# Two transformer blocks on one core: routing on unscaled rows, a slot table in memory, gather and sum by matrix products, and the second projection in the same program block

## The chip, the cores and the metric

The kernel runs on one core of a Trainium2 chip. The metric is device time in microseconds (us). TensorE does the matrix products (PE in the rows, its weight loads PEld), VectorE (DVE), ScalarE (ACT) and GpSimd (POOL) the elementwise work, and SyncE (SP) issues most transfers. All data are float32.

## The reference

512 tokens of width 1024 pass through two blocks. In each: RMS norm, an input projection, a mixer (stick-breaking attention and RWKV-7 in the first, HGRN2 and forgetting attention in the second), an output projection added to the residual, RMS norm, and a mixture of experts with a two-level router. After the experts there is a final RMS norm; that of the first block feeds the second block. The experts and what stands on both sides of them are what changes:

```
h  = h + mixed @ w_out
xn = rmsnorm(h, norm_ffn_g)
# router: softmax over 4 groups of (xn @ w_grp + b_grp), best group;
#         in it the best two experts of (xn @ w_exp + b_exp), with weights
for e in range(N_EXPERTS):
    y = y + combine[:, e:e+1] * ((silu(xn @ w_gate[e]) * (xn @ w_up[e])) @ w_down[e])
h = rmsnorm(h + y, final_norm_g)
# second block: u = rmsnorm(h, attn_norm_2) @ w_in_2, and so on
```

The first block has 32 experts with a hidden width of 256, the second 16 with 512. Either way a block reads 100.7 MB of expert weights.

## The kernel before

The phases run one after the other, each in a program block of its own with a barrier of all engines behind it: first projection (`phase_project1`), attention, RWKV, the expert block (`expert_block`), second projection (`phase_project2`), HGRN2, forgetting attention, the expert block again.

An expert block is made of three parts. `out_programs` projects with w_out, four token tiles of 128 rows by two halves of 512 columns, on TensorE; VectorE adds to the residual `z.h`; ScalarE squares the row, takes a root, and writes the scaled row `z.xn` in a permuted order of columns, which TensorE turns (`turn`) into `mixT`; TensorE multiplies with the router weights (`route`). A chain of small VectorE instructions picks group and experts, and TensorE counts the rank of each token in its expert (`z.q`).

`moe_programs` (first block) and `wide_programs` (second block) then run eight bodies each. The weights of a body (12.6 MB: four experts or two) stand in one buffer per expert, and a buffer's next load is issued by SP when the body's product with it is done; the gate and up weights are freed by `gate_up`, the down weights by `down`. A body's 256 slots (four experts by 64) or 192 slots (two by 96) are found by a one-hot matrix `z.G` on VectorE and a product with the token numbers on TensorE (`index_pe`); GpSimd fetches the rows by an indirect transfer from memory (`fetch_rows`); TensorE turns them (`turn_rows_pe`) and VectorE writes them with the gain (`turned_rows_dve`). Rows of the body after next are fetched while a body runs. ScalarE copies each output and stores all slots, full or empty, in memory (`expert_rows`). The bodies are a hardware loop of six passes and two more behind it; a branch over further rounds, for more tokens than slots, follows.

`final_programs` starts after the last body's stores: GpSimd fetches each token's two rows with eight indirect transfers, VectorE multiplies and adds them, and the final norm follows. After the first block, its result is stored, the engines meet at the barrier, and `phase_project2` norms the rows again, turns them (`norm_turn_pe`) and projects (`project_pe`).

## Time and profile before

| | us |
|---|---|
| median of 3 runs (1667.97 to 1669.82) | 1669.01 |
| the profiled execution, its own time | 1672.01 |
| its span, first to last instruction | 1670.3 |
| mean granted TensorE clock | 0.903 of full |
| PE busy | 1399.1 (84%) |
| DVE busy | 424.3 (25%) |
| ACT busy | 354.1 (21%) |
| POOL busy | 158.4 (9%) |
| moved by DMA | 287.34 MB, mean 172 GB/s |

The busy share of 84% is a mean over stages: the two blocks' stages each have their own limit, and the rows further down are therefore cut by stage. The PE row counts the time in which a product runs, whatever the clock; a product of a 128x128 tile with 512 columns in float32 is two instructions.

### The profile page before, as it was taken

To read this page: it belongs to the slowest core of one execution; us is meant where nothing else is said; L and a number is where in the kernel's file an instruction comes from. 1 tells how busy PE (TensorE), PEld (TensorE's weight loads), DVE (VectorE), ACT (ScalarE), POOL (GpSimd) and SP (SyncE) were. 2 spreads that over 40 slices of the span, in tenths; PEclk is the share of its full clock that TensorE was granted. 3 is DMA by queue.
4 is the path that set the end of the run, shared out by engine and by line. 5 is a ranking of instruction groups with operands and counts; after the bars stand their busy time and mean duration, and the time that the engine had idled before them with its cause. 6 is when DMAs were issued, how large, how long until landed. Compare 5 with 4: busy or idle time off the path is not lost. (4 is left out here: it accounts for less than half of the span.)

```text
span 1670.3 us, 23492 instructions
## 1 busy us (share of the span) xinstructions
PE 1399.1 (84%) x9946; PEld 701.0 (42%) x9946; DVE 424.3 (25%) x827; ACT 354.1 (21%) x615; POOL 158.4 (9%) x217
## 2 busy tenths in 40 slices
PE   5999989877896988778089999577889799999991
PEld 3434444677455433232044444466545433333320
DVE  2234325422214111101421000682512311111003
ACT  2023026342211111101221100323522011111101
POOL 4000002252001001000100000240000000000001
PEclk8989999999995989989599999786999699999996
DMA  5111100200425899998523210002052389989944
GB/s 190 51 51 51 50 0 0 103 4 4 147 100 200 357 419 418 418 416 332 179 105 119 76 51 0 1 1 71 31 216 115 112 336 358 363 347 358 372 186 171
DMA packets 70007, 287.34 MB, mean 172 GB/s; under 512 B 11475, under 2 KB 12570, under 8 KB 57634
## 3 DMA queue, kind: packets, MB, share of 16 engines
q1 hardware_dynamic: 57088, 250.41, 38.5%
q0 software_dynamic: 6400, 16.79, 3.0%
q10 hardware_dynamic: 6434, 18.92, 2.9%
q8 instruction: 64, 1.05, 0.3%
q14 instruction: 21, 0.17, 0.0%
HBM read 269.30 MB, written 23.07 MB: 175 GB/s over the span
## 5 line engine op out<-in xcount | busy, mean ns | idle before, releaser
L344 PE MATMUL banks<-mixT,ring 128*128 128x512 f32 x672 | 294.9, 601 | 3.8 <-DVE mixT L285 3.8
L344 PEld LDWEIGHTS banks<-mixT,ring 128*128 128x128 f32 x672 | 129.3, 193 | 168.6 <-issue 164.4
L1922 PE MATMUL banks<-arena_moe,mixT 128*32 128x512 f32 x768 | 173.7, 600 | 0.0
L1922 PE MATMUL banks<-ring,mixT 128*32 128x512 f32 x768 | 117.2, 617 | 5.7 <-DMA arena_moe<-in_w_up 4.8
L1372 PE MATMUL banks<-ring,mixT 128*128 128x512 f32 x256 | 114.4, 607 | 8.0 <-PEq L51 8.0
L1558 POOL DMA_INDIRECT arena_moe<-normed_rows,arena_moe x32 | 32.8, 1025 | 745.9 <-DVE arena_moe L1586 605.7
L1749 PE MATMUL banks<-arena_moe,mixT 128*64 128x512 f32 x256 | 70.2, 709 | 37.6 <-DMA arena_moe<-in_exp_w_up 37.6
L341 PE MATMUL banks<-ring,mixT 128*128 128x512 f32 x192 | 82.9, 592 | 0.0
L1372 PEld LDWEIGHTS banks<-ring,mixT 128*128 128x128 f32 x256 | 49.4, 195 | 69.5 <-issue 69.5
L1922 PEld LDWEIGHTS banks<-ring,mixT 128*32 128x32 f32 x768 | 34.0, 114 | 86.3 <-issue 86.3
L1749 PE MATMUL banks<-ring,mixT 128*64 128x512 f32 x256 | 60.0, 623 | 6.8 <-DMA ring<-in_exp_w_up 5.6
L1609 DVE TENSOR_TENSOR mixT<-banks,params 128x512 f32<-128x512 f32 (+1 forms) x64 | 38.7, 622 | 102.5 <-PE banks L1600 102.5
L2001 DVE TENSOR_TENSOR mixT<-mixT,banks 128x256 f32<-128x256 f32 x24 | 10.1, 421 | 197.6 <-ACT mixT L2029 197.6
L1922 PEld LDWEIGHTS banks<-arena_moe,mixT 128*32 128x32 f32 x768 | 43.8, 109 | 35.1 <-issue 35.1
L1749 PEld LDWEIGHTS banks<-arena_moe,mixT 128*64 128x64 f32 x256 | 22.9, 162 | 84.7 <-issue 84.7
L1944 PE MATMUL banks<-ring,mixT 128*32 128x512 f32 x384 | 56.5, 594 | 0.5 <-ACT mixT L2033 0.5
L1944 PE MATMUL banks<-arena_moe,mixT 128*32 128x512 f32 x128 | 56.4, 593 | 0.0
L341 PEld LDWEIGHTS banks<-ring,mixT 128*128 128x128 f32 x192 | 36.5, 190 | 45.9 <-issue 45.9
L1600 PE MATMUL banks<-ident,arena_moe 128*128 128x128 f32 (+1 forms) x256 | 49.8, 300 | 6.3 <-DMA arena_moe<-normed_rows,arena_moe 6.3
L2186 ACT ACTIVATE arena_mix<-banks 128x512 f32<-128x512 f32 x28 | 16.7, 597 | 176.8 <-PE banks L344 129.8
L1807 DVE TENSOR_TENSOR mixT<-mixT,banks 128x256 f32<-128x256 f32 x16 | 6.7, 421 | 184.1 <-ACT mixT L1835 184.1
L462 ACT ACTIVATE arena_mix<-banks 128x512 f32<-128x512 f32 x26 | 15.5, 597 | 174.0 <-PE banks L344 148.9
(392 smaller groups left out, 1925.5 us busy)
## 6 DMA issues: line engine op xcount, KB each, us to landing
ring<-in_w_in SPq DMA_DIRECT2D x18, 1024.0 KB, 7.5
arena_moe<-in_exp_w_gate SPq DMA_DIRECT2D x16, 1024.0 KB, 18.8
arena_moe<-in_exp_w_up SPq DMA_DIRECT2D x16, 1024.0 KB, 23.1
arena_moe<-in_exp_w_down SPq DMA_DIRECT2D x16, 1024.0 KB, 21.6
ring<-in_exp_w_gate SPq DMA_DIRECT2D x16, 1024.0 KB, 16.1
ring<-in_exp_w_up SPq DMA_DIRECT2D x16, 1024.0 KB, 18.0
ring<-in_exp_w_down SPq DMA_DIRECT2D x16, 1024.0 KB, 23.0
arena_moe<-in_w_gate SPq DMA_DIRECT2D x8, 2048.0 KB
```

The lines of the kernel that those rows point to most:

```text
L341: last = pe.matmul(bank[:, 0:4 * P], m.mixT[:, c, i * P:(i + 1) * P], w[:, c, 0:4 * P], start=(c == 0), stop=(c == DC - 1))
L344: last = pe.matmul(bank[:], w[:, c, i * P:(i + 1) * P], m.mixT[:, c, :], start=(c == 0), stop=(c == DC - 1))
L462: act.activation(out, bank, ACT.Copy, scale=scale).then_inc(ph.sem("taken"), 1)
L1372: last = pe.matmul(m.banks[k % 3][:], m.mixT[:, c, i * P:(i + 1) * P], w[:, c, :], start=(c == 0), stop=(c == DC - 1))
L1558: pool.indirect_dma_start(z.xs[0:count, c, :], None, z.normed, bass.IndirectOffsetOnAxis(ap=z.index[0:count, c:c + 1].bitcast(U32), axis=0 ...
L1600: last = pe.transpose(pair[a][:, at:at + count], z.xs[0:count, c, j * P:(j + 1) * P], m.ident[0:count, 0:count])
L1609: dve.tensor_tensor(z.xe[:, j:j + 2, :], pair[a][:, 0:2 * z.slots].rearrange("p (j n) -> p j n", j=2), m.params[:, gain + j:gain + j + 2]. ...
L1749: last = pe.matmul(hb[u][k * cap:(k + 1) * cap, :], z.xe[:, j, s * cap:(s + 1) * cap], both[:, :, j, :], start=(j == 0), stop=(j == DC - 1))
L1922: last = pe.matmul(hb[u][T * i:T * (i + 1), :], z.xe[:, j, at:at + T], both[:, :, j, half * 256:half * 256 + 256], start=(j == 0), stop=(j ...
L1944: last = pe.matmul(yb[n][T * i:T * (i + 1), :], z.hT3[:, h, f, T * i:T * (i + 1)], wd[:, 2 * half + f, n * HW:(n + 1) * HW], start=(h == 0 ...
L2001: dve.tensor_tensor(z.hid3[:, u, :], z.hid3[:, u, :], hb[u][:, 256:512], ALU.mult).then_inc(ph.sem("hidden_done"), 1)
L2186: act.activation(out, bank[:], func, scale=scale).then_inc(ph.sem("taken"), 1)
```

## The change

In words, by part:

- **First projection.** GpSimd makes a blank; SP writes two tables of slots and two output arrays of 4.2 MB with it (`clear_exchange`), behind the loads of the third weight item. Two more gain vectors are loaded by ScalarE.
- **Before the experts.** TensorE turns the unscaled rows `z.h`, so `turn` and `route` no longer wait for the row's norm; the gain is multiplied into the router's weights, the scale and the bias are applied to the logits of each tile. ScalarE and VectorE also split the normed row into a rounded part `x_hi` and its rest `x_lo`, in the type F32R.
- **Slots.** The per-body one-hot, `index_pe` and `index_dve` are gone. One one-hot is built for the first body. GpSimd writes, by eight indirect transfers, for each token and choice a pair (row number, weight) into a table in memory; SP reads the whole table back, four transfers in pieces of 8 bytes; GpSimd turns it into row numbers.
- **First body.** TensorE gathers the rows as a product of `x_hi` and `x_lo` with the one-hot (`gather_pe`, 64 products).
- **Bodies 1 to 7.** Rows are fetched by the table. ScalarE applies the weight when it copies the output, and waits for the table before the first body's work. GpSimd scatters the outputs of bodies 0 to 6 by indirect transfers to token order (`place_rows`), only full slots. The bodies are written out; the branch for further rounds now stands ahead of body 0.
- **End.** The outputs of bodies 0 to 6 are loaded in token order while the last body runs (`load_outputs`), VectorE adds them (`early`), the last body's outputs are split into `y_hi` and `y_lo` and summed by TensorE (`sums_pe`, 32 products), and VectorE adds the banks.
- **Second projection** runs in the same program block; its first weights are asked for while the last body runs. `between_programs` computes both norms in one go: two squares, a root and two scaled copies per tile on ScalarE.

The core of the diff:

```
+    pool.memset(x.zeros, 0.0).then_inc(ph.sem("blank"), 1)
+    pool.iota(x.blank, [[0, P], [-NOWHERE, 2]], base=NOWHERE, channel_multiplier=0).then_inc(ph.sem("blank"), 1)
...
+def clear_exchange(sp, ph, x, exchanges):
+
+    sp.wait_ge(ph.sem("blank"), 2)
+    for d in exchanges:
+        sp.dma_start(d.outputs.rearrange("(p a) (b n) -> p (a b) n", p=P, n=512), x.zeros.unsqueeze(1).broadcast_to([P, 16, 512])).then_inc(ph.sem("cleared"), 16)
+        n = d.table.shape[0] // P
+        sp.dma_start(d.table.rearrange("(p n) v -> p n v", p=P), x.blank[:, 0:n, :]).then_inc(ph.sem("cleared"), 16)
...
+            act.wait_ge(ph.sem("cleared"), 32 * len(exchanges))
...
+        parts = m.open(f"moe{block}", {"x_hi": (NT, D), "x_lo": (NT, D), "G": (NT * 256,)})
+        self.x_hi, self.x_lo = parts["x_hi"], parts["x_lo"]
+        self.G = parts["G"][:, 0:NT * self.slots].rearrange("p (t n) -> p t n", t=NT)
+        self.ST = parts["G"][:].rearrange("p (c s) -> p c s", c=2)
...
+        spent = m.ring01[:, 0, 0:NT * D] if self.wide else self.ring23[:, 0, 0:NT * D]
+        self.outs = (spent.rearrange("p (t d) -> p t d", d=D), self.xn)
...
+    def load_slots(self, sp, slots, first_rank, sem):
+
+        t = self.d.table.rearrange("(i e n) v -> e i n v", e=self.EB, n=self.d.entries)
+
+        def part(partition, c, e, rank, n):
+            src = t[e][:, bass.ds(first_rank + rank, n), :].rearrange("i n v -> n i v")
+            sp.dma_start(slots.raw[partition:partition + n, :, c, :], src).then_inc(sem, 16)
+
+        if self.wide:
+            part(0, 0, 0, 0, self.cap)
+            part(self.cap, 0, 1, 64, self.cap - 64)
+            part(0, 1, 1, 0, 64)
+            part(64, 1, 1, 0, 64)
+        else:
+            for e in range(4):
+                part(64 * (e % 2), e // 2, e, 0, 64)
...
+        pe.wait_ge(ph.sem("wr_scaled"), 1)
         for i in range(1, NT):
-            project(i)
-            if i >= 2:
-                route(i - 2)
+            project(i, 0, every)
             turn(i - 1)
-        route(NT - 2)
+            project(i, 1, front)
+            route(i - 1)
+            project(i, 1, back)
         turn(NT - 1)
         route(NT - 1)
 
...
+            act.activation(z.x_hi[:, i, :], z.xn[:, i, :], ACT.Copy).then_inc(ph.sem("high"), 1)
...
+        def split(t_):
+
+            dve.wait_ge(ph.sem("high"), t_ + 1)
+            dve.tensor_tensor(z.x_lo[:, t_, :], z.xn[:, t_, :], z.x_hi[:, t_, :].bitcast(F32), ALU.subtract).then_inc(ph.sem("split"), 1)
...
+        dve.tensor_tensor(z.wr[:, :, 0:G + E], z.wr[:, :, 0:G + E], m.params[:, gain:gain + DC].unsqueeze(2).broadcast_to([P, DC, G + E]),
+                          ALU.mult).then_inc(ph.sem("wr_scaled"), 1)
...
+    def gpsimd(pool):
+
+        pool.iota(z.count, [[1, S]], base=0, channel_multiplier=0).then_inc(ph.sem("ramp"), 1)
+        pool.wait_ge(ph.sem("ramp"), 1)
+        pool.tensor_copy(z.ramp, z.count).then_inc(ph.sem("ramp"), 1)
+        pool.wait_ge(ph.sem("entries"), 2)
+        for t_ in range(NT):
+            for k in range(2):
+                pool.indirect_dma_start(z.d.table, bass.IndirectOffsetOnAxis(ap=z.position[:, k, t_:t_ + 1].bitcast(U32), axis=0),
+                                        z.entry[:, k, t_, :], None, bounds_check=E * z.d.entries - 1,
+                                        oob_is_err=False).then_inc(ph.sem("tabled"), 16)
...
+def gather_pe(pe, ph, z, banks):
+
+    for b in range(4):
+        for j in (2 * b, 2 * b + 1):
+            at = (j % 2) * z.slots
+            for t in range(NT):
+                for part in (z.x_hi, z.x_lo):
+                    last = pe.matmul(banks[b][:, at:at + z.slots], part[:, t, j * P:(j + 1) * P], z.G[:, t, :],
+                                     start=(t == 0 and part is z.x_hi), stop=(t == NT - 1 and part is z.x_lo))
+        last.then_inc(ph.sem("gathered"), 1)
...
+def sums_pe(pe, ph, m, z, t, c, last_part):
+
+    for n in range(2):
+        for part in (z.y_hi, z.y_lo):
+            if z.wide and c == 1:
+                a, b, y = 64 * n, 64 * n + 64, part[64 * n:64 * n + 64, 2, :]
+            else:
+                a, b, y = 0, P, part[:, 2 * c + n, :]
+            last = pe.matmul(m.banks[2 * t + n][:], z.ST[a:b, c, t * P:(t + 1) * P], y,
+                             start=(c == 0 and part is z.y_hi), stop=(c == 1 and part is z.y_lo), skip_group_check=True)
+    if last_part:
+        last.then_inc(ph.sem("summed"), 1)
+
+
+def all_sums_pe(pe, ph, m, z, first, both):
+
+    pe.wait_ge(ph.sem("chosen_slots"), 2)
+    pe.wait_ge(ph.sem("y_low"), first)
+    for t in range(2):
+        sums_pe(pe, ph, m, z, t, 0, False)
+    pe.wait_ge(ph.sem("y_low"), both)
+    for t in range(2):
+        sums_pe(pe, ph, m, z, t, 1, True)
+    for t in range(2, NT):
+        for c in range(2):
+            sums_pe(pe, ph, m, z, t, c, c == 1)
...
+def load_outputs(sp, ph, z):
+
+    sp.wait_ge(ph.sem("hidden"), z.units * (z.bodies - 1) + 2)
+    sp.wait_ge(ph.sem("placed"), 32 * (z.bodies - 1))
+    for t in range(NT):
+        for k in range(2):
+            sp.dma_start(z.outs[k][:, t, :], z.d.outputs[k * S + t * P:k * S + (t + 1) * P, :]).then_inc(ph.sem(f"outputs{t}"), 16)
...
+        sp.wait_ge(out.sem("tabled"), TABLED)
+        z.load_slots(sp, z.main, 0, ph.sem("slots"))
+        further.run(sp, begin, body, lambda n: body(n * NB, 0))
+        load_gain()
+        for i in range(1, NB):
+            for s in range(4):
+                sp.wait_ge(ph.sem("hidden"), 2 * i + s // 2 - 1)
                 z.load_in(sp, io, s, i, ring_sems[s])
             for s in range(4):
-                sp.wait_ge(ph.sem("down"), g * 2 + s // 2 - 1)
+                sp.wait_ge(ph.sem("down"), 2 * i + s // 2 - 1)
                 z.load_down(sp, io, s, i, ring_sems[4 + s])
-
-        with sp.Fori(1, NB) as i:
-            fill(i, i)
-        sp.wait_ge(out.sem("rounds"), 1)
-        n = sp.value_load(m.rounds[0:1, 0:1], min_val=1, max_val=rounds.most)
-        with sp.If(n > 1):
-            with sp.Fori(1, n) as r:
-                with sp.Fori(0, NB) as i:
-                    fill(r * NB + i, i)
-        with sp.Else():
-            sp.nop()
+        load_outputs(sp, ph, z)
...
+        further_pool(pool, further, z, x, out, 4)
+        pool.wait_ge(ph.sem("slots"), 64)
+        slots_known(pool, z, z.main, ph.sem("known"), 0)
+        fetch_rows(pool, ph, z, z.main.fetch[:, 1, :])
+        for i in range(NB - 1):
+            pool.wait_ge(ph.sem("y_taken"), 4 * i + 2)
+            place_rows(pool, ph, z, z.main.place[:, i, :], 0)
+            if i + 2 < NB:
+                pool.wait_ge(ph.sem("gathered"), 4 * (i + 1) + 4)
+                fetch_rows(pool, ph, z, z.main.fetch[:, i + 2, :])
+            pool.wait_ge(ph.sem("y_taken"), 4 * i + 4)
+            place_rows(pool, ph, z, z.main.place[:, i, :], 1)
...
+        chosen_slots_dve(dve, ph, z)
+        hidden(ph, NB - 1, 0)
+        hidden(ph, NB - 1, 1)
+        for c in range(2):
+            for n in range(2):
+                y_low_dve(dve, ph, z, 2 * c + n, yb[2 * c + n], z.main.weight[:, NB - 1, c:c + 1])
+        for t in range(NT):
+            early(t)
...
+        act.wait_ge(ph.sem("slots"), 64)
+        for i in range(NB - 1):
+            hiddens(ph, i)
...
+        def squares(t):
+            act.wait_ge(experts.sem("total"), t + 1)
+            act.activation(store[:, t, :], z.h[:, t, :], ACT.Square, accum_out=stat(t, S1)).then_inc(ph.sem("squares"), 1)
+            act.wait_ge(ph.sem("gained"), t + 1)
+            act.activation(m.rows[:, t, :], hg[:, t, :], ACT.Square, accum_out=stat(t, S2)).then_inc(ph.sem("squares"), 1)
+
+        def root(t):
+            act.wait_ge(ph.sem("means"), t + 1)
+            act.activation(stat(t, D1, 2), stat(t, MS1, 2), ACT.Sqrt).then_inc(ph.sem("deviations"), 1)
+
+        def scale(t):
+            act.wait_ge(ph.sem("inverses"), t + 1)
+            act.activation(scaled[:, t, :], hg[:, t, :], ACT.Copy, scale=stat(t, BOTH)).then_inc(ph.sem("scaled"), 1)
+            act.activation(store[:, t, :], hg[:, t, :], ACT.Copy, scale=stat(t, I1)).then_inc(ph.sem("unscaled"), 1)
+            act.wait_ge(ph.sem("unscaled"), t + 1)
+            act.dma_start(rows[:, t, :], store[:, t, :]).then_inc(ph.sem("stored"), 16)
+
+        for t in range(NT):
+            squares(t)
+            root(t)
+            if t:
+                scale(t - 1)
+        scale(NT - 1)
+        act.wait_ge(ph.sem("stored"), 16 * NT)
+        p_scalar(act)
...
+        for t in range(NT):
+            add_sums_dve(dve, experts, m, z, t)
+            gained(t)
+            if t:
+                means(t - 1)
+            if t >= 2:
+                inverses(t - 2)
+        means(NT - 1)
+        inverses(NT - 2)
+        inverses(NT - 1)
+        dve.wait_ge(ph.sem("squares"), 2 * NT)
+        for t in range(NT):
+            taken(t)
...
```

## Rows read from the trace of the kernel before

**Rows 1.** Windows by stage: PE, PEld, DVE, ACT, POOL busy, clock, DMA share, GB/s.

```profile
564.90:778.70 213.80, 170.54 (x812) 70.00 (x809) 27.17 (x55) 29.54 (x55) 10.98 (x11) 0.91 1.02 418
...
1283.80:1320.90 37.10, 25.11 (x133) 21.47 (x132) 13.21 (x48) 6.37 (x8) 1.99 (x2) 0.57 0.56 213
1320.90:1634.00 313.10, 307.30 (x2560) 104.92 (x2560) 36.46 (x100) 37.01 (x77) 13.61 (x14) 0.95 0.81 313
1634.00:1670.30 36.30, 0.00 (x0) 0.00 (x0) 16.16 (x20) 6.93 (x14) 8.15 (x8) 0.55 0.50 181
```

**Rows 2.** Timeline of block 1 between its projection and its first body.

```profile
499.46 1.87 PE L1392 MATMUL banks<-arena_moe,mixT 128*128 128x36 f32 x16
...
512.60 0.31 DVE L1473 TENSOR_TENSOR arena_moe<-banks,arena_moe 128x144 f32<-128x144 f32 x1 [3.72 <-PE banks L1392]
...
518.44 0.80 PE L1409 MATMUL banks<-arena_moe,after 128*128 128x128 f32 x2 [5.88 <-DVE arena_moe L1491]
...
520.80 1.29 DVE L1801 TENSOR_TENSOR arena_moe<-slots,arena_moe 128x512 f32<-128x512 f32 x2
...
538.05 8.86 PE L1749 MATMUL banks<-ring,mixT 128*64 128x512 f32 x32 [1.20 <-DVE arena_moe L1586]
```

**Rows 3.** TensorE's timeline in block 1: bodies 0, 1 and 7.

```profile
553.98 1.04 PE L1600 MATMUL banks<-ident,arena_moe 128*128 128x128 f32 x8
...
559.68 1.84 PE L1577 MATMUL banks<-tokens,arena_moe 128*128 128x1 f32 x16
...
564.94 7.03 PE L1749 MATMUL banks<-ring,mixT 128*64 128x512 f32 x32
...
778.66 9.72 PE L1749 MATMUL banks<-arena_moe,mixT 128*64 128x512 f32 x32 [4.96 <-DMA arena_moe<-in_exp_w_up]
```

**Rows 4.** SP's queue in block 1: the first refill of a weight buffer.

```profile
547.09 0.35 SPq L1317 DMA_DIRECT2D ring<-in_exp_w_gate  x1
```

**Rows 5.** GpSimd's row fetches (L1558): ns of one, and us from issue to landing.

```profile
L1558 POOL DMA_INDIRECT arena_moe<-normed_rows,arena_moe x32: 931/991/1517, 526.7 to 1556.1; - x32
...
DMA to landing us min/median/max: 4.3/8.3/9.1
```

**Rows 6.** The router's small loads (L1351): ns of an issue, and us to landing.

```profile
L1351 SPq DMA_DIRECT2D arena_moe<-in_router_exp_w x1: 3607/3607/3607, 440.3 to 440.3; - x1
...
DMA to landing us min/median/max: 8.3/8.3/8.3
```

**Rows 7.** Timeline at the end of block 1 and start of the second projection.

```profile
797.42 0.60 ACT L1847 ACTIVATE arena_moe<-banks 128x512 f32<-128x512 f32 x1 [1.12 <-PE banks L1769]
...
809.49 1.28 DVE L1634 SCALAR_TENSOR_TENSOR arena_moe<-arena_moe 128x1024 f32<-128x1024 f32 x1 [18.98 <-DMA mixT<-expert_rows,arena_moe]
...
812.13 1.06 ACT L248 ACTIVATE arena_moe<-arena_moe 128x1024 f32<-128x1024 f32 x1 [12.27 <-DVE arena_moe L1634]
...
844.97 55.61 PE L344 MATMUL banks<-mixT,ring 128*128 128x512 f32 x125 [3.82 <-DVE mixT L285]
```

**Rows 8.** Chain that ended last, in block 2's bodies 0 and 1.

```profile
1320.87 16.82 PE banks L1922 x128
...
1362.93 13.73 PE banks L1922 x128
...
1384.67 16.29 DMA arena_moe<-in_w_up
```

**Rows 9.** Timeline at the end of block 2.

```profile
1622.57 0.17 DVE L1617 TENSOR_SCALAR arena_moe<-arena_moe 128x8 f32<-128x8 f32 x1 [0.15 <-issue]
...
1633.97 0.60 ACT L2040 ACTIVATE arena_moe<-banks 128x512 f32<-128x512 f32 x1 [3.27 <-PE banks L1956]
...
1662.55 1.29 DVE L1677 SCALAR_TENSOR_TENSOR mixT<-arena_moe,small 128x1024 f32<-128x1024 f32 x1
```

**Rows 10.** The start: the last gain vectors on ScalarE's queue, and TensorE's wait.

```profile
18.59 0.58 ACTq L167 DMA_DIRECT2D arena_mix<-in_fox_norm  x2
...
24.05 0.37 PE L572 MATMUL banks<-ident,arena_mix 64*128 64x64 f32 x1 [7.07 <-DMA arena_mix<-in_fox_norm]
```

1125 lines of the change are left out of this document (630 added, 495 removed).

## The prediction

> **What bounds the kernel now.** I read the busy time of each engine by stage first, because the page's 84% for TensorE hides the places where it stands. In the windows [rows 1] look at the DMA column against the PE column. In block 1, from 564.9 to 778.7, the transfers run at a share of 1.02 and 418 GB/s while TensorE is busy for 170.5 of 213.8 us: the weights set that stage. In block 2 the same column is 0.81 and TensorE is busy for 307.3 of 313.1 us: TensorE sets it, with the weights close behind. The window behind the last body, 36.3 us, has no product at all.
>
> Next the timelines at the four seams, where one engine waits for another. Between block 1's last projection product and its first body lie 499.46 to 538.05, 38.6 us [rows 2]; in block 2 it is 37.1 us [rows 1]. Between block 1's last output copy, 797.42, and the first product of the second projection, 844.97, lie 47.5 us [rows 7]; behind block 2's last copy, 1633.97, the last row is scaled until 1663.84, 29.9 us, and its store ends the span at 1670.3 [rows 9]. Together 153 us, and the change works on all of them. Last I read the chain inside block 2's bodies: body 1 ends not on a product but on a weight load of 16.29 us that starts when the third gate product is done [rows 8].
>
> **The seam ahead of block 1's bodies.** T is the end of the last projection product. One `route` (1.87 us) moves ahead of it, so T = 499.46 + 1.87 = 501.3. After T: an add of 0.7, half a turn and two copies, 2.4 in all; the last `route` 1.9; logits 0.3: T+4.8. The picking chain is the same, 512.60 to 518.44 less its first 0.3, 5.5 us [rows 2]: T+10.3. Counting and `z.q` took 518.44 to 520.80, 2.4 us; the last split (one pass over 1024 columns, 1.28 [rows 7]) lies beside it. The one-hot is 1.29: T+14. Before, the same point was 499.46+22.6, so seven microseconds come from unscaled routing (8.6 less the moved route).
>
> Then `gather_pe`, 64 products in the type F32R, which no row shows. From below: an instruction with a short moving side took 1.84/16 = 0.115 us [rows 3], so 64 x 0.115 = 7.4. From above: a float32 product of 512 columns is two instructions of 55.61/125 = 0.445 [rows 7], so 256 columns as float32 cost 0.44, and 64 of them 28; with block 2's 192 columns, 21. TensorE comes out of a wait, with a granted clock of 0.57 over the seam [rows 1], which cost 16.82 - 13.73 = 3.1 us on a body's first products [rows 8]; I add 2. I take 9.4 in block 1. In block 2 I take 16, halfway, because its moving side is shorter and I can't exclude that it loses the fast pace.
>
> The Trainium skill, "FP8 and Floating Point Precision", section "TensorE Precision Notes", says that true float32 takes four passes and names a reduced-precision read that isn't split. By it the 512-column product is a quarter of 0.89; no row here shows the reduced kind. By one pass the sum gains 6.6 us more in block 2's gather; by four it loses what the second rival says.
>
> So body 0 could start at T+25. But it needs the table. `position` and weights come some 2.2 us behind the one-hot, T+16.2; GpSimd starts 1 us later and issues eight scatters, 0.99 with 0.30 between, the last at T+26.3; landing 4.3 at best [rows 5]: T+30.6. Behind it SP reads the table, 2048 pieces of 8 bytes. The nearest row is the router's load of 1,024 pieces, issued behind another 1,024 and landed 8.3 after issue [rows 6]; I take 8.9: T+39.5. SP is through at about T+38, ScalarE waits for the table before its first `silu`, GpSimd then needs 1.5 for the row numbers, 1 to start, 1.3 and 8.3 to land under load: rows at T+51.6. TensorE wants them behind both gate products, T+41. A stall of 10.6 us, which is new. What is queued behind it on TensorE is both `down` products, and behind those SP's reload of the down buffers. From the turn on, body 0 took 553.98 to 564.94, less the 1.84 of `index_pe` [rows 3], plus 2 for a slow restart: body 1 starts at T+62.8 = 564.1, against 564.94. TensorE has gained nothing here.
>
> **Block 1's bodies.** The transfers decide. Their stream starts when SP is free, T+38 = 539.3, against 547.09 [rows 4]: 7.8. In body 0 they run dry near T+68: -2. Seven bodies stored 256 slots each, 7.3 MB; 128 of them are full on average (1,024 choices over 8 bodies), so the scatter writes 3.7 MB less, at 418 GB/s 8.8 us. The last gate product, 778.66 [rows 3], comes 14.6 earlier.
>
> **The seam behind block 1.** T0 is the last `down`. Splitting the last bank is 0.6 on ScalarE and 0.75 on VectorE: T0+1.5. VectorE's queue then holds eight adds of 1.28, 10.3 us, before it may add TensorE's sums: T0+11.9. They hide the 32 products of `sums_pe` (6.8 from a quarter of 0.89; 28 if not). Then each tile costs ScalarE two squares of 1.06+0.19, a root 0.2, two copies of 1.05 and a store 0.4: 5.2, four times 20.9; the first add, waits for VectorE's small instructions in between, and the last tile's turn and copies make 27.8. The projection starts at T0+39.7, against 47.5: gain 7.8. Its weights are in by then, as before.
>
> **Block 2.** Gather from T+13, so body 0 at 13+16+0.6, and 1 for reading the round count: T+30.5, and T is 1.9 later: 32.4 against 37.1, gain 4.7. The third gate product of body 0 covers the rows' landing. Body 0 saves 3.1 of slow start and 1.7 of `index_pe`: 4.8. Bodies 1 to 6 save 1.7 where TensorE sets the period and 0.6 where the weight load does; of the six I put three at each, 7. The end: T0+1.5, four sums 0.9, then four tiles of 1.28 add and 1.28 scale with the last square and root behind, T0+14.9 against 29.9: 15.0, since the early adds lie in the last body. Sum 31.5.
>
> **Small terms.** Two more vector loads at 0.3 each delay the wait that holds TensorE until 24.05 [rows 10]: +0.65. More semaphores to free: +0.5. The 8.6 MB of blanks go out in a projection that moves 50 GB/s. The branch over the rounds now stands before body 0. The row for such a branch is 0.15 us on VectorE [rows 9], and I cost it at nothing. The Trainium skill, "Runtime: NRT & Kernel Launch", "Instruction fetch mechanics", warns that a taken branch can force a fetch and stall; here the trace disagrees in size, with 0.15.
>
> **Sum.** -14.6 - 7.8 - 31.5 + 1.15 = -52.8. The profiled execution's own time is 1672.01 (span 1670.3 and 1.7 around it), the median 1669.01; 1669.0 - 52.8 = 1616.
>
> **Rivals.**
> (a) Gains as forecast: 1616, chance 0.60, own range 1606 to 1628.
> (b) F32R runs as slowly as float32. Block 1's gather is 19 longer, of which the row stall takes all but 5; block 2's costs 7 more; its sums 28 instead of 6.8, +20; behind block 1 the sums outlast the adds, +10. 1658. For it: no row of the type; against: nothing in the trace. 0.10.
> (c) The table is read slowly: twice the 8.9 taken from the router's row is +9 in block 1, where the weight stream waits with it, and +6 in block 2, behind the third gate product: 1631. For it: the pieces are smaller than the router's, and more of them stand in one transfer; against: the router's own are small too. 0.17. The Trainium skill, "DMA: Bandwidth & Descriptors", sections "Specifications" and "Bandwidth", puts pieces under 512 bytes in a slow class and a packet at about 10.5 ns; an estimate by that page is 21.5 us for 2048 pieces, and a sum of 1638.
> (d) Scatters disturb the weight stream so that the 8.8 us aren't saved: 1625; 0.07.
> (e) The other side: the table path decides alone. In each block everything from the scatter on shifts one for one once it is past the cover; it cancels 53 us when scatter and table take about 27 us longer per block, so 49 instead of 22. At 25 ns a piece the table takes 51, 42 more in each block, and with 3 of it covered in block 2 the time is 1697. The router's rows speak against it. 0.05. The rest, 0.01, is no change: gains at the seams that the rows' stalls give back exactly.
>
> Range: 1602 to 1640. It holds (a), (d) and (c); (b) and (e) stay out. A change within 0.2% (3.3 us) can't be told from none. Faster 0.94, within 0.01, slower 0.05.
>
> **What would show it.** In the profile after: first body 25 to 31 us behind the last projection product; in block 1 a wait of TensorE for the fetched rows in body 0, near 10 us, and the DMA column still at 1.0 through the bodies, about 205 us long instead of 213.8; in block 2 periods of 37.6 instead of 39.3; VectorE adding for 10 us behind block 1's last `down`; 15 us from block 2's last copy to the last scaled row. The forecast is wrong if the table lands later than 12 us behind the last scatter, if a gather product takes over 0.3 us, or if the DMA share in block 1 falls below 0.95, because then the stream isn't what holds the bodies.

## The result, and the profile after

The changed kernel took 1647.05 us (median of four runs, 1644.19 to 1649.94) against 1669.41 in the same session: a ratio of 0.9866, 95% interval 0.9846 to 0.9886. A repeat on another chip gave 0.982 (0.9793 to 0.9847). So it is 22 to 30 us faster. The prediction was 1616 us and its range ended at 1640: the direction was right, the size about twice too large (52.8 us forecast; by the medians 22.4 and 28.2).

The windows of the changed kernel by stage. Rows answer to those in [rows 1]; the third to the sixth are block 1's seam, body 0 up to the first weight refill, the rest of body 0, and the bodies behind it; the last five are the stretch between the blocks, block 2's seam, its body 0, its bodies 1 to 6, and the end.

```profile
core 0: us, PE busy (x) PEld busy (x) DVE busy (x) ACT busy (x) POOL busy (x), PEclk, DMA share, GB/s
444.54:509.39 64.85, 64.85 (x202) 33.02 (x203) 15.17 (x31) 14.93 (x16) 1.18 (x2) 0.97 0.43 157
509.39:536.04 26.65, 16.36 (x105) 15.46 (x103) 15.60 (x52) 6.17 (x8) 7.20 (x8) 0.74 0.67 257
536.04:550.68 14.64, 14.64 (x62) 5.71 (x64) 0.00 (x0) 1.28 (x1) 0.83 (x1) 0.88 0.06 4
550.68:578.36 27.68, 12.66 (x59) 5.48 (x57) 3.42 (x6) 3.27 (x7) 4.92 (x10) 0.69 0.98 379
578.36:782.80 204.44, 162.57 (x730) 61.01 (x727) 21.54 (x39) 25.34 (x50) 24.83 (x25) 0.91 1.02 414
...
840.13:1223.15 383.02, 327.85 (x1313) 185.83 (x1313) 114.20 (x225) 91.57 (x178) 28.81 (x28) 0.91 0.11 39
1287.82:1315.19 27.37, 17.97 (x105) 17.23 (x103) 13.63 (x53) 6.19 (x8) 7.91 (x8) 0.68 0.65 251
1315.19:1354.66 39.47, 37.58 (x311) 12.33 (x312) 3.50 (x7) 5.46 (x10) 6.71 (x12) 0.96 0.71 259
1354.66:1587.69 233.03, 219.46 (x1860) 75.90 (x1861) 21.78 (x44) 25.08 (x54) 22.67 (x23) 0.99 0.93 355
1624.51:1648.20 23.69, 6.76 (x33) 4.00 (x32) 11.51 (x17) 5.77 (x13) 0.00 (x0) 0.74 0.22 89
```

Two things stand out. From 536.04 to 550.68 TensorE works and the transfers stand still, 4 GB/s, in a block that the transfers set (before, the first refill stood at 547.09, and ahead of it the transfers were slow too, 66 GB/s from 538 to 547). And in block 2 TensorE is busy for 219.46 of 233.03 us: about 2 us in each body are now missing that were not missing before. The waits of TensorE name both:

```profile
engine line waited for: us in total, times, longest us
PE banks L1891 <- DMA arena_moe<-in_exp_w_up: 34.1, 6, 6.7
...
PE banks L2144 <- DMA arena_moe<-in_w_up: 15.5, 7, 2.8
PE banks L2722 <- PEq L51: 13.2, 1, 13.2
PE banks L1731 <- DMA arena_moe<-normed_rows,arena_moe: 13.0, 1, 13.0
```

The wait for in_w_up is block 2's (4.8 us in three waits before). The 13.0 us is the new wait for fetched rows in block 1's body 0. Where the gain came from and where it went, by the mean of two profiles of each kernel (the profiled executions above and the two repeats):

| stage | before | changed | difference | forecast |
|---|---|---|---|---|
| ahead of block 1's projection | 439.3, 441.1 | 444.5, 440.7 | +2.4 | +1.15 |
| block 1, first projection product to last `down` | 358.1, 355.4 | 357.2, 356.5 | +0.1 | -14.6 |
| seam behind it | 47.6, 47.7 | 38.4, 38.4 | -9.3 | -7.8 |
| second projection to block 2's | 378.6, 378.5 | 383.0, 383.6 | +4.8 | 0 |
| block 2, first projection product to last `down` | 410.4, 408.4 | 401.4, 400.6 | -8.4 | -16.5 |
| end | 36.4, 36.5 | 23.7, 23.7 | -12.8 | -15.0 |
| sum | | | -23.2 | -52.8 |

Half of the miss is in block 1, which gained nothing; a quarter is in block 2; most of the rest lies at phase changes, which the sum priced at 0.5 us.

### The profile page after: what moved, and what is told of

Same layout as the page of the kernel before. It is cut to its first block and busy times, and to the rows that moved or that the text cites. A ratio compares the mean times of both kernels' runs of the same rounds, so it can differ in the third digit from the quotient of the medians.

```text
span 1648.2 us, 22613 instructions
## 1 busy us (share of the span) xinstructions
PE 1389.2 (84%) x9850; PEld 696.6 (42%) x9850; DVE 428.0 (26%) x797; ACT 363.0 (22%) x617; POOL 188.7 (11%) x259
## 5 line engine op out<-in xcount | busy, mean ns | idle before, releaser
L2144 PEld LDWEIGHTS banks<-ring,mixT 128*32 128x32 f32 x768 | 37.9, 114 | 95.9 <-issue 95.9
L1703 POOL DMA_INDIRECT expert_rows<-arena_moe x21 | 21.1, 1006 | 404.3 <-PE banks L1731 188.3
L344 PEld LDWEIGHTS banks<-ring,mixT 128*128 128x128 f32 x192 | 36.5, 190 | 45.9 <-issue 45.9
L1731 PE MATMUL banks<-ident,arena_moe 128*128 128x128 f32 x224 | 41.5, 289 | 13.0 <-DMA arena_moe<-normed_rows,arena_moe 13.0
## 6 DMA issues: line engine op xcount, KB each, us to landing
ring<-in_exp_w_down SPq DMA_DIRECT2D x16, 1024.0 KB, 22.4
```

Source lines behind the costliest of these rows:

```text
L344: last = pe.matmul(bank[:, 0:4 * P], m.mixT[:, c, i * P:(i + 1) * P], w[:, c, 0:4 * P], start=(c == 0), stop=(c == DC - 1))
L1703: pool.indirect_dma_start(z.d.outputs, bass.IndirectOffsetOnAxis(ap=place[:, c:c + 1].bitcast(U32), axis=0), z.y[:, 2 * c:2 * c + 2, :].re ...
L1731: last = pe.transpose(pair[a][:, at:at + count], z.xs[0:count, c, j * P:(j + 1) * P], m.ident[0:count, 0:count])
L2144: last = pe.matmul(hb[u][T * i:T * (i + 1), :], z.xe[:, j, at:at + T], both[:, :, j, half * 256:half * 256 + 256], start=(j == 0), stop=(j ...
```

## The experiments

Each experiment was timed beside the kernel before on the same chip; `spaced` and the second profile of before have one run each. Medians differ by chip, so ratios are compared. But the changed kernel itself gave 0.9866 and 0.982, 7.5 us apart, so a ratio of 0.979 to 0.989 alone doesn't tell a variant from it. Stage lengths tell more. The same seam behind block 1 took 38.35 to 38.38 us in eleven profiles; an unchanged block 1 took 356.2 to 358.0 in five, and an unchanged block 2 mostly 400.4 to 401.4, but 396.0 to 397.8 in three.

**The changed kernel once more.**

> The changed kernel as it is, timed beside the others of this call, and a second profile of it. Noise theory: about 4 us of the 5.3 us that its first profile lost ahead of the first expert block came from a fall of the granted clock to 0.50 at 244 to 250 us and should not stand at that place again, while the 3.5 us longer gap at the phase change near 1050 us, where an instruction fetch stands in the records, comes back, since the program is the same. Rival, the loss belongs to the new instructions: both are there again. Time 1644 to 1650.

Measured: 1644.13 us, ratio 0.982. The projection started at 440.68, the fall of the clock at 244 us was not there, the phase change near 1050 again took 5.63 us. Over the fourteen profiles of the changed kernel and its variants the projection starts anywhere between 437.4 and 444.5. The two of the changed kernel alone differ by 3.9 us (granted clock from 240 to 255 us 0.66 and 1.00), so most of the 5.3 us can be where the clock's falls lay; that is inferred. At the start TensorE's wait for the last vector ended at 25.53 and 25.45 instead of 24.05 and 24.69: 0.8 to 1.5 us, against 0.65 forecast.

**Who issues the table's load.**

```diff
-        sp.wait_ge(out.sem("tabled"), TABLED)
-        z.load_slots(sp, z.main, 0, ph.sem("slots"))
+        act.wait_ge(out.sem("tabled"), TABLED)
+        z.load_slots(act, z.main, 0, ph.sem("slots"))
```

> Edit: ScalarE instead of SP waits for the scattered slots and issues the loads of the table, in both blocks; SP goes straight to its next weight loads. Stream theory: block 1 is as long as its weight stream from its first refill on (231.6 us before, 232.1 after), so what counts is when that starts; it starts at about 544 to 545, when the first gate products are done, instead of 550.68. Then block 1's last gate product comes about 5 to 6 us earlier and the time is 1641 to 1643. The table then lands under load, so rows and with them body 1's start come later by up to 5 us, at no cost. Row theory: the wait of 12.98 us for the fetched rows in body 0 decides; then moving the stream ahead gives nothing or costs up to 5 us: 1647 to 1652. In block 2 both expect no change within 1 us.

Measured: 1660.71, ratio 0.9922 (0.9892 to 0.9952). Block 1 became 14.7 us longer (371.6 against 356.9), so both theories fail. The stream did start early, at 541.68 where the changed kernel's started at 550.68, but the table's small pieces now stood among the weights. These are windows of this kernel:

```profile
core 0: us, PE busy (x) PEld busy (x) DVE busy (x) ACT busy (x) POOL busy (x), PEclk, DMA share, GB/s
545.00:550.00 5.00, 3.52 (x18) 1.08 (x14) 0.00 (x0) 0.00 (x0) 0.00 (x0) 1.00 1.01 390
...
560.00:565.00 5.00, 0.00 (x0) 0.00 (x0) 0.00 (x0) 0.00 (x0) 0.00 (x0) 0.50 1.02 399
565.00:570.00 5.00, 0.69 (x2) 0.29 (x2) 0.75 (x2) 1.04 (x3) 1.35 (x7) 0.50 0.18 20
570.00:575.00 5.00, 0.00 (x0) 0.00 (x0) 0.00 (x0) 0.00 (x0) 1.95 (x2) 0.50 0.41 112
575.00:580.00 5.00, 4.18 (x14) 2.34 (x16) 1.38 (x2) 0.00 (x0) 0.00 (x0) 0.50 0.00 2
580.00:585.00 5.00, 5.00 (x26) 2.07 (x24) 0.85 (x2) 1.29 (x3) 0.00 (x0) 0.83 0.10 9
```

The stream fills every free buffer by 565 and then is nearly dry until 585, but for a burst behind 570: the table came at 567.56, ScalarE waited for it ahead of its first `silu`, `down` waited behind both, and the buffers' reloads behind `down`. So the row path costs nothing only as long as the stream has buffers to fill. That is the condition the next experiment has to be read with.

**Both down products ahead of the rows' turns in body 0.**

```diff
+            if i == 0:
+                down(ph, i, 0, ring_sems)
+                turn_hidden(ph, i, 1)
+                down(ph, i, 1, ring_sems)
+                turn_rows_pe(pe, ph, m, z, gath, 0, 32, None)
+                turn_rows_pe(pe, ph, m, z, gath, 1, None, 4)
+                return
```

> Edit: in block 1's body 0 TensorE does both down products ahead of the turns of the next rows, so the 12.98 us wait for the fetched rows no longer holds the down products nor the reload of the down buffers; body 1 can start at about 573 instead of 578. Row theory: the wait in body 0 is on the path, and the time falls by 4 to 5 us, to about 1642. Stream theory: the transfers run without a hole from 555 on either way and set the end of the stage, so body 1 starts earlier only to wait more for its weights, and the time stays within 1 us of the changed kernel's.

Measured: 1643.37, ratio 0.9818, no difference. Body 1 started 61.0 us behind the last projection product instead of 69, and block 1 took 354.9 us instead of 356.9: of 8 us that the body came earlier, 2 were left at its end. The stream theory holds in the changed kernel.

**The 3.67 MB that are no longer written.**

```diff
+                act.dma_start(z.d.more[(2 * i + c) * 64:(2 * i + c) * 64 + 64, :],
+                              z.y[0:64, 2 * c:2 * c + 2, :].rearrange("p i n -> p (i n)")).then_inc(ph.sem("more"), 16)
```

> The changed kernel with one thing added: in block 1's bodies 0 to 6 ScalarE also stores 64 of the 128 rows of each half of the output to a spare tensor, 14 x 256 KB, 3.67 MB, which is what the scatter no longer writes. The result stays. Bytes theory: the weight stream sets the stage from its first refill on, and 3.67 MB at 418 GB/s make block 1 8.8 us longer. Rival: the fewer bytes never counted, and the stage grows by under 3 us.

Measured: 1649.91, ratio 0.9881 (0.9854 to 0.9908), block 1 363.8 us, 6.9 more than the 356.9. Bytes count, at 6.9 us for 3.67 MB where the forecast had 8.8. (One profile. The added stores also make ScalarE wait for one transfer more, which this run doesn't separate from the bytes.)

**The table in rank order.** Experts h x 16 + c x 8 + i for body i, and the entry at rank x 32 + expert:

```diff
-        dve.tensor_tensor(z.position, z.rank, z.first_entry, ALU.add)
+        dve.scalar_tensor_tensor(z.position, z.rank, float(E), z.first_entry, ALU.mult, ALU.add)
-            for e in range(4):
-                part(64 * (e % 2), e // 2, e, 0, 64)
+            for h in range(2):
+                part(64 * h, None, h, 0, 64)
```

> Edit: the slot table lies rank by rank, and a body takes experts from both halves of the list, so that each partition's entries are contiguous: block 1 reads its table as 128 pieces of 128 bytes in two loads, not 2048 pieces of 8 bytes in four. The work is the same. Theory, the table path decides block 1's body 0 and holds the weight stream behind it: the table lands 3 to 4 us after issue instead of 7.4, rows and body 1 come 4 to 5 us earlier, the first refill 2 to 3 us earlier, and block 1's last gate product 3 to 5 us earlier; block 2 gains under 1 us. Time 3 to 5 us below the changed kernel's. Rival, the landing is set by the transfer's fixed time and by the scatters before it and not by the count of pieces: landing stays above 6 us and the time within 1 us.

Measured: 1636.71, ratio 0.9791 (0.9771 to 0.9812). Block 1 took 347.4 us, 9.5 less, twice what was expected, and the reason was not the one given. (By the whole time the gain is within what two sessions of one kernel differ by; the table's path below is far outside it.) First the timeline of the changed kernel:

```profile
535.90 0.97 POOL L1638 DMA_INDIRECT slot_table<-arena_moe  x1 [0.30 <-issue]
545.45 3.17 SPq L1388 DMA_DIRECT2D arena_moe<-slot_table  x4
550.28 0.35 SPq L2438 DMA_DIRECT2D arena_moe<-in_final_norm_g  x1
550.68 0.43 SPq L1374 DMA_DIRECT2D ring<-in_exp_w_gate  x1
...
552.88 0.20 POOL L1675 CAST arena_moe<-arena_moe 128x16 f32<-128x16 int32 x1 [16.00 <-DMA arena_moe<-slot_table]
```

and that of the kernel in rank order:

```profile
533.92 0.97 POOL L1646 DMA_INDIRECT slot_table<-arena_moe  x1 [0.30 <-issue]
537.24 1.16 SPq L1396 DMA_DIRECT2D arena_moe<-slot_table  x2
539.78 0.20 POOL L1683 CAST arena_moe<-arena_moe 128x16 f32<-128x16 int32 x1 [4.88 <-DMA arena_moe<-slot_table]
541.35 0.33 SPq L1380 DMA_DIRECT2D ring<-in_exp_w_gate  x1
```

The number in brackets is the whole path from GpSimd's last scatter to the table on chip: 16.00 us became 4.88. Of the 11 us, 6.2 lie ahead of the load's issue (from the scatter's end, 536.87 to 545.45, 8.6; here 2.35): the scatters land sooner, and nothing about the read explains that. Over the nine profiles in which block 1's table stood as in the changed kernel this gap was 6.6 to 8.6 us and the path 14.7 to 17.3.

**Rank order, but read in 8-byte pieces.**

```diff
-        self.flat, at = m.view(at, 2, bodies, 2, dt=I32)
+        self.raw, at = m.view(at, bodies, 2, 2, dt=I32)
```

> The packed table's order of experts and places in memory, but the entries of a partition lie apart on chip as in the changed kernel, so each transfer again consists of 8-byte pieces (four loads of 512 pieces). Tells apart what the packed table's gain of 10 us in block 1 came from. Pieces theory: reading in small pieces costs twice, in the 6 to 8 us between the last scatter and the first load and in the landing; both come back, block 1 is as long as in the changed kernel (about 292 us from its last projection product to its last down product, packed 281.9), and the time is about 8 to 10 us above the packed kernel's. Rival, the scatters into rank order land faster or the order of experts helps: the gap stays at 2.4 us and the gain is kept by more than half.

Measured: 1636.96, ratio 0.9793; the path took 6.11 us, block 1 353.1. The rival holds for the path: with the same 2048 pieces most of its gain stays, and the reading in few pieces is worth 1.2 us of it. For block 1 it isn't settled: it kept 3.8 of its 9.5 us in this profile, less than half, and the whole kernel all of it.

**Entries 64 bytes apart.**

```diff
-            (experts * self.entries, 2), I32
+            (experts * self.entries * 8, 2), I32
-        dve.tensor_tensor(z.position, z.rank, z.first_entry, ALU.add)
+        dve.scalar_tensor_tensor(z.position, z.rank, 8.0, z.first_entry, ALU.mult, ALU.add)
```

> The changed kernel with one size changed: the table's entries stay in expert order and are read in the same 2048 pieces of 8 bytes, but stand 64 bytes apart in memory instead of 8 (the table is 8 times as long and its clearing writes 8 times as much). In the changed kernel the scatters land 7.1 us after issue in the median, the last 9.5, and the first load of the table is issued 6.5 to 8.6 us behind the last scatter; in the kernel in rank order it is 1.8 to 2.4 us. Neighbour theory: 8-byte writes that stand next to each other in memory hold each other up; then the gap falls to about 2 us with spacing alone, the loads land 2.3 us after issue instead of 4.1, and block 1 (from its first projection product to its last down product, 356.5 to 357.2) is 4 to 9 us shorter. Rival, something else in the order of addresses: gap and landing stay.

Measured (one run): 1640.1. Expert order, 2048 pieces, and yet:

```profile
532.76 0.97 POOL L1639 DMA_INDIRECT slot_table<-arena_moe  x1 [0.30 <-issue]
535.56 2.70 SPq L1389 DMA_DIRECT2D arena_moe<-slot_table  x4
539.95 0.20 POOL L1676 CAST arena_moe<-arena_moe 128x16 f32<-128x16 int32 x1 [6.22 <-DMA arena_moe<-slot_table]
540.31 0.43 SPq L1375 DMA_DIRECT2D ring<-in_exp_w_gate  x1
```

Path 6.22 us, loads landing 2.3 us after issue, block 1 351.3 us. So it is the addresses of the 8-byte writes that decide, and not how the table is read. That neighbouring entries wait for each other doesn't follow, though: in rank order entries of one rank stand 8 bytes apart too, and in block 2 of the changed kernel itself, where the table is in expert order with neighbours 8 bytes apart, the path is short:

```profile
1312.77 0.98 POOL L1638 DMA_INDIRECT slot_table<-arena_moe  x1 [0.30 <-issue]
1315.14 3.43 SPq L1388 DMA_DIRECT2D arena_moe<-slot_table  x4
1320.37 0.20 POOL L1675 CAST arena_moe<-arena_moe 128x16 f32<-128x16 int32 x1 [6.62 <-DMA arena_moe<-slot_table]
```

Here the load is issued 1.4 us behind the scatter's end, against 8.6 in block 1. Between the two tables the number of experts differs, and the distance from one expert's entries to the next: 4096 bytes in block 1 (512 entries), 4608 in block 2 (576), 32768 in the spaced table. No run changed that distance alone, so it stays a rival. The Trainium skill, "DMA: Bandwidth & Descriptors", section "Specifications", says that transfers below 512 bytes are done as a read, a change and a write. All these writes are of 8 bytes, the fast ones too, so that alone doesn't tell them apart. Why block 1's are slow stays open.

**Block 2's weights in column halves.**

```diff
+                    cols = slice(256 * half, 256 * half + 256)
+                    sp.dma_start(both[:, k][:, :, cols], w[:, :, cols]).then_inc(done, 16)
```

> Edit: block 2 loads the gate and up weights of each expert in column halves with a semaphore for each half; the first gate product waits for the first halves only, the second for the second halves. Load theory: in block 2 each body waits for the load issued behind its third gate product (16 to 17 us to landing, TensorE idle 15.5 us in seven bodies, and slower products behind four of these waits); with the first halves in 5 us earlier the wait is gone, periods fall from 38.8 to 36 to 37, and the time falls by 13 to 18 us, to about 1632. Rival, the transfers themselves are the limit or smaller pieces (1 KB rows instead of 2 KB) slow them: landing grows, and the time falls by under 3 us or rises.

Measured: 1654.25, ratio 0.9893 (0.9864 to 0.9922): slower by 10 us, block 2 411.4 us against 401. The rival's second half holds, with other sizes than I gave. Unsplit, the rows of a partition lie one behind another, so that gate and up weights move in packets of 16 KB; halved by columns, in packets of 1 KB. Both kernels from 1354 to 1580 us, the changed one first:

```profile
DMA packets 12236, 79.89 MB, mean 353 GB/s; under 512 B 1674, under 2 KB 1674, under 8 KB 9255
```

```profile
DMA packets 53331, 76.20 MB, mean 337 GB/s; under 512 B 1852, under 2 KB 45744, under 8 KB 53316
```

While full of weights the queue moved 347 to 358 GB/s here, 418 to 441 in the changed kernel, and an issue on SP took mostly 2.9 us, up to 5.2, instead of 0.4.

**The same waits, with long pieces.**

```diff
+                    js = slice(4 * half, 4 * half + 4)
+                    sp.dma_start(both[:, k, js], w[:, js]).then_inc(done, 16)
...
+                if u == 0 and j == 4:
+                    for s in range(2):
+                        pe.wait_ge((z.x_late if ring is x_ring else z.late)[s], 32 * g + 32)
```

> Edit: block 2 loads gate and up weights of each expert in two transfers again, but cut along the contraction, so that the pieces keep their full rows; the first gate product waits for the first four chunks only, and for the rest in its middle. Availability theory: the column halves lost because 1 KB pieces ran at about 348 GB/s instead of 427, and not because earlier availability is worth nothing; with long pieces the waits of 1.8 to 2.8 us ahead of each body go (TensorE idle 15.5 us in seven bodies), periods come to 36 to 37 us, and block 2 is 12 to 17 us shorter. Rival, the transfers as a whole limit block 2: the waits move into the middle of the product, and the block gains under 3 us.

Measured (packets of 8 KB, 413 to 428 GB/s while full): 1627.0, ratio 0.9737 (0.972 to 0.9754). Block 2 took 381.5 us, 19.5 less, more than the theory's 12 to 17. Its bodies 1 to 6 in the windows:

```profile
core 0: us, PE busy (x) PEld busy (x) DVE busy (x) ACT busy (x) POOL busy (x), PEclk, DMA share, GB/s
1354.00:1570.00 216.00, 216.00 (x1876) 71.95 (x1872) 21.77 (x44) 25.51 (x55) 22.72 (x23) 1.00 0.99 382
```

TensorE is never idle, the granted clock stays at 1.00, and every period is 35.82 us; the changed kernel's six were 37.81 to 40.40. The two longest of those hold a wait and, behind it, two gate products in 15.6 us instead of 13.95: a wait of 2.5 to 2.8 us was followed by a stretch with a lower granted clock (0.88 from 1466 to 1480), so that it cost more than its length.

**The seam behind block 1.**

```diff
+            add_outputs_dve(dve, experts, z, t)
             add_sums_dve(dve, experts, m, z, t)
```

> Edit: behind block 1 VectorE adds the stored rows tile by tile, each tile's two adds just ahead of its add of TensorE's sums, instead of all eight first; and ScalarE loads its table of functions one copy later in the last body. Theory: ScalarE, which needs 5.9 us for each tile, starts after 2.4 + 1.2 us of adds instead of 9.7 + 1.2, so the second projection starts 5 to 6 us earlier behind the last down product, and the 1.85 us that TensorE waits in the last body falls by about 1.3. Together 6 to 7 us. Rival: VectorE's 5.7 us for each tile becomes the bound or the stored rows are not in yet at 803, and the gain is under 3 us.

Measured: 1638.68, ratio 0.9806. The seam shrank from 38.37 to 36.30 us only: the rival, in a form of its own. ScalarE began its first square 5.2 us behind the last `down` instead of 12.3, but then stood between its tiles, for example

```profile
807.46 0.20 ACT L2357 ACTIVATE arena_moe<-arena_moe 128x2 f32<-128x2 f32 x1 [4.46 <-DVE arena_moe L2383]
```

because VectorE's small means of a tile now queued behind 4.9 us of large adds of the next (2.48 + 1.22 + 1.23). With the means moved between (below) the seam took 32.60. The later load of ScalarE's table gave 1.3 us as expected: TensorE's wait of 1.85 us became 0.52.

**Without the further rounds.**

```diff
         engine.wait_ge(self.known, 1)
+        return
         n = engine.value_load(self.m.rounds[0:1, 0:1], min_val=0, max_val=z.most - 1)
```

> Leaves out the further rounds (no value load, no branch, no code for them), which this input doesn't take, so the result stays. Theory: the 3.17 and 3.34 us in which TensorE stands ahead of body 0 are the value load and the branch over that code; the copies of the gathered rows end 0.3 to 0.5 us behind the last gather product, so body 0 starts 2.3 to 2.7 us earlier in each block, and the smaller program also takes away part of the 5.45 us gap at the phase change near 1050 us. Time 4 to 7 us lower. Rival: in block 1 the earlier start only lengthens the wait for the rows, and the gap stays: 2 to 3 us lower.

Measured: 1638.51, ratio 0.9806 (0.9789 to 0.9823). In block 1 TensorE still waited 2.68 us between the last gather product and body 0, where it waited 3.17 in the changed kernel and 3.31 in its repeat, so the theory that the branch is this wait fails. But the branch isn't cheap. In the trace's sequencer records, which the views don't list, the compare and branch over the further rounds takes 4.45 and 4.61 us on TensorE in the two blocks of the changed kernel (4.58 and 4.39 in its repeat, 3.6 to 4.8 in the kernel before, there off the path), and 0.05 to 0.07 us on each other engine; every one of TensorE's has one packet of an instruction queue in it. I had read its price from VectorE's row. In the first profile body 0 waited for the branch's end: the copy was done at 533.6, the branch at 535.88. VectorE's last two copies of gathered rows in this kernel (start, length, then in brackets the idle time before it and what ended that):

```profile
529.12 0.69 DVE L1741 TENSOR_TENSOR mixT<-banks,params 128x512 f32<-128x512 f32 x1 [1.23 <-issue]
532.89 0.69 DVE L1741 TENSOR_TENSOR mixT<-banks,params 128x512 f32<-128x512 f32 x1 [3.08 <-remote]
```

The last one starts 1.9 us behind the product that it waits for, which ended at 531.00; body 0 follows 0.1 behind the copy. In the repeat of the changed kernel the copy was 2.4 us late, while the first three of the series start at once. In the changed kernel's own first profile it started at once, and the 2.4 us came behind it. In block 2 the wait was even 4.65 us here. I forecast 0.6 for it, and 1 in block 2 for the branch. With the branch gone the last product's signal still came 1.9 us late in block 1; why taking it out gave back at most 0.6 us is open. The phase change near 1050 shrank from 5.62 to 4.33 us.

**A second profile of the kernel before.**

> The kernel before as it is, for a second profile of it. In fourteen profiles of the changed kernel and its variants block 1's projection starts between 437.4 and 444.5; before it started at 439.28. If the extra loads and the clearing cost the first phases 5 us, this one starts near 439 again or earlier; if most of that was the placing of the granted clock's falls, it can start anywhere up to 443. The stretch between the second projection's start and block 2's projection took 378.6 us, against 381.3 to 384.5 in the others, with a gap of 2.12 us at the phase change near 1055 where they show 5.62; both should come back.

Measured: start of the projection 441.09, the stretch between the blocks 378.5, the phase change 2.11. The rows of before and of the changed kernel:

```profile
1055.96 0.48 DVE L2252 MEMSET arena_mix<- 128x512 f32 x1 [2.12 <-PEq L51]
```

```profile
1054.79 0.48 DVE L2607 MEMSET arena_mix<- 128x512 f32 x1 [5.62 <-PEq L51]
```

So 3.5 us there are a real cost of the change. What fills the gap are instructions that no view lists and the trace holds: while the other engines wait, GpSimd clears the semaphores of the phases that have ended, one clear behind the other.

| | before | changed | without further rounds |
|---|---|---|---|
| gap near 1050, us | 2.12 | 5.62 | 4.33 |
| clears in it, and us from first to last | 4, 1.21 | 25, 4.73 | 20, 3.44 |
| clears at the last phase end, us | 19, 3.20 | 31, 5.53 | 24, 3.93 |

Each clear takes 0.17 to 0.19 us. Thirteen of those near 1050 stood in the seam behind block 1 before (2.58 us there), since the second projection now shares its program block; the rest belong to semaphores that the change added. The prediction weighed the Trainium skill, "Runtime: NRT & Kernel Launch", section "Instruction fetch mechanics", which says that a taken branch to a page outside the current window stalls the engine for a fetch, and set it aside. TensorE's branch, with its 3.6 to 4.8 us and a packet of an instruction queue in each, agrees with the page. The phase change doesn't need it: a packet lies in that gap too, but the largest hole between two clears is 0.35 us, as it was before (0.36).

**All together.** Rank order, long chunks, adds tile by tile with the means between, and the later table loads:

> Packed table, block 2's chunked waits, and behind block 1 the adds tile by tile with the small means moved between the stored rows' adds and the sums, ScalarE scaling a tile ahead of the next root; the load of ScalarE's square root table one copy later in both last bodies. If the parts add up: 10 in block 1, 19 in block 2, 2 to 6 behind block 1, 2 to 3 in the last bodies, so 33 to 38 below the changed kernel: 1608 to 1614. Rival, they share their causes (each removes waits behind the same transfers): less than 28, above 1617.

Measured: 1610.34 (1603.6 to 1614.83), ratio 0.9627 (0.9598 to 0.9655) to the kernel before: 60 us faster than it. The parts add up within what the stages scatter by. Block 1 349.7 (7.1 of the 9.5 us kept, in one profile), seam 32.60, block 2 380.9.

> The same with block 1's body 0 doing both down products ahead of the turns of the next rows. Stream theory: body 0's wait for the rows (7 us with the packed table) stands on nothing that sets the end; within 1 us of the kernel without it. Row theory: 3 to 5 us less.

Measured: 1609.47, ratio 0.9632: the same by the whole time. Block 1 took 345.6 us in its one profile, 4.1 less, so a small gain isn't excluded.

## Why the prediction was wrong

**Block 1 up to its last gate product, -14.6; measured +0.1** (to the last `down`; to the start of the last gate product, which the term speaks of, -0.4). This is the step that failed most, in three terms.
First, "Their stream starts when SP is free, T+38 = 539.3 ... : 7.8". Counted from the first projection product the first refill of before came at 107.8 us; the changed kernel's at 106.1 and 104.0, so 1.7 to 3.8 us earlier. The counting error was mine: two `route`s and a turn moved ahead of T, not one `route`, which made T 2.7 us later. The rest is the table path: scatters taken as landing in 4.3 us took 8.6 and 6.9 to the load's issue, and the table was on chip 16.0 and 15.2 us behind the last scatter. The prediction had named that as its sign of being wrong, "later than 12 us". Its other two signs didn't show (a gather product 0.12 to 0.21 us, DMA share 1.02).
Second, the stall: rows at T+58.1 instead of T+51.6, body 1 at T+69.0 instead of T+62.8. By itself it cost nothing much (down_first), as I had reckoned for the wrong reason.
Third, "the scatter writes 3.7 MB less, at 418 GB/s 8.8 us". Bytes count (more_bytes, 6.9 us), but the stretch from first refill to last `down` was 250.3 us before and 251.1 and 252.5 after; with rank order it was 248.5. Up to the start of the last gate product 96.0 MB went through in 231.6 us before, 95.1 MB in 232.1 us after. Fetches and stores fell by 3.0 MB, not 3.7; the stream took up 0.52 MB of the gain vector and some 1.5 MB more of weights; and the mean rate fell from 414 to 410 GB/s. By that rate the four are an estimate of 1.6, 1.2, 3.6 and 2.3 us, together 8.7 of the 9.3 us missing. The saving was spent by bytes that the term didn't count. The last body holds besides a wait of TensorE of 1.85 us for ScalarE's table load, which stood in no term.

**Ahead of block 1, +1.15; measured +2.4**, of which 0.8 to 1.5 us is seen at the start; the rest is within what two profiles of one kernel differ by.

**Seam behind block 1, -7.8; measured -9.3.** Right: the projection started 38.4 us behind the last `down` against a forecast of 39.7. VectorE's ten microseconds of adds stood there as predicted (9.66).

**Block 2, -16.5; measured -8.4.** Gather: 16 us taken, 10.7 measured. Body 0 started 27.4 us behind the last projection product; the seam gained 5.5 against 4.7, with one `route` more ahead of T here as well. Body 0 gained 2.6 instead of 4.8: of the 3.1 us "of slow start" its first product saved 1.3 (9.96 to 8.63), and nothing in the repeat (10.03). Bodies 1 to 6 gained 1.2 instead of 7. That was the failing term: "of the six I put three at each". All of them ran into the load issued behind the third gate product, which landed 16 us later and made a period of 37.8 at best. I had [rows 8] with that very chain in hand, and priced the body by the mean of two bounds instead of asking which ends last once the shorter one shrinks. The experiment with chunks shows what TensorE alone takes: 35.82.

**The end, -15.0; measured -12.8.** VectorE was through 14.9 us behind the last `down`, exactly the sum; the 2.3 us lost are GpSimd's clears at the last phase end, 31 in 5.53 us instead of 19 in 3.20. **Between the blocks, 0; measured +4.8**, 3.5 of it the phase change near 1050 and 0.7 the clears at two other phase ends. "More semaphores to free: +0.5" was the right mechanism with the wrong size: it measured about 6.5 us.

**The rivals.** (b) is refuted: 64 products of type F32R with 256 columns took 9.1 us (10.5 in the repeat), one 0.12 us behind the other at the upper level of the clock and 0.21 at the lower, a quarter of float32's price. The Trainium skill, "FP8 and Floating Point Precision", section "TensorE Precision Notes", gives true float32 four passes; it gives no number for the reduced read, and the measured price fits one. (c), the table read twice as slowly (1631), named the right path with the wrong end of it: the read took 7.4 us instead of 8.9, the scatters ahead of it 8.6 and 6.9 instead of 4.3. The estimate of 21.5 us for 2048 pieces, by the Trainium skill, "DMA: Bandwidth & Descriptors", section "Bandwidth", is far from the 7.4 measured. (d), the 8.8 us not saved, describes block 1 but not why: more_bytes shows that bytes count. The range failed because it held each rival alone; the phase changes and block 2's load stood in none. Three sums don't come out of their own terms, by little: T+4.8 should be 4.6 or 5.3; (b)'s 19 us less what the row stall takes leave 8.0 and not 5; and 32 products at a quarter of 0.89 are 7.1, not 6.8 (measured 7.55).

## What to carry to other kernels

Where two waits of almost equal length alternate at setting a loop's period, the shorter path's gain is nil until the other is moved as well; here splitting one wait along the contraction, with the pieces kept long, was worth 19.5 us, nearly as much as the whole change. A small table that the engines write and read back through memory is a path of its own: price its scatter, its landing and what stands behind it in the same queue, and try another order of its entries, since here the order alone was worth 10 us of the path. Each semaphore that a kernel allocates is cleared at a phase end while every engine waits, so count them. And read the price of a branch on the engine whose branch is on the path.

## What the runs showed of the hardware

Eight scatters of 128 entries of 8 bytes each, in a table with 4096 bytes from expert to expert, held the reader for 6.6 to 8.6 us behind the last; with 4608 bytes, with entries 64 bytes apart, or in rank order it was 1.2 to 2.4 us. Weights in packets of 1 KB moved at 347 to 358 GB/s, in packets of 8 or 16 KB at 413 to 441. An F32R product of 192 columns took 0.111 us at the upper and 0.213 at the lower clock, hardly less than one of 256 columns (0.12 and 0.21). The branch over the further rounds took TensorE 3.6 to 4.8 us and the other engines 0.05 to 0.07. GpSimd's clears at a phase end took 0.17 to 0.19 us each, one behind the other.
